# A two-layer hybrid trunk: the attention probabilities turned by VectorE instead of by TensorE, and the steps around them placed later

## The chip, the cores and the metric

The kernel runs on one core of a Trainium2 chip. The metric is the device time of one execution in microseconds (us), as the median of several. Engines are named as in the profile: PE is TensorE's matmuls, PEld its weight loads, DVE is VectorE, ACT is ScalarE, POOL is GpSimd, SP is the engine that issues the weight transfers.

## What is computed

Two layers, 256 tokens, model width 2048, everything float32. The part that matters here, per layer:

```python
h = rms_norm(x, pre_g)
proj = h @ w_in                       # 2048 x 24576: 12 mixer sections of 1536, 3 gates of 2048
o_a = dilated_mixture_attn(q_a, k_a, v_a) * silu(z_a)      # 12 heads x 128
o_c = b_c * causal_short_conv(c_c * u_c, conv_w, conv_b) * silu(z_c)
o_r = retention(q_r, k_r, v_r) * silu(z_r)                 # 12 heads x 128
merged = (sigmoid(g_a) * (o_a @ w_branch_a) + sigmoid(g_c) * (o_c @ w_branch_c)
          + sigmoid(g_r) * (o_r @ w_branch_r))
x = x + rms_norm(merged @ w_out, post_g)
```

The mixture of three dilated attentions is computed as one softmax over all keys, with the logarithm of how many of the three patterns hold a pair added to its score. For one head that is a causal 256 x 256 matrix, kept as three blocks of 128 x 128: queries 0 to 127 on keys 0 to 127, and queries 128 to 255 on both halves of the keys.

## The kernel before

**Weights.** All weights stream through SBUF once a layer, in blocks of 512 columns. A block of `w_in` is 16 tiles of 128 rows. The unit of the whole schedule is a *half*: two such tiles, 128 x 1024 numbers. Each half is split into two fp32r parts, whose sum is the float32 weight: ScalarE copies the rounded value into `w_lead` (L644), VectorE subtracts to get the rest into `w_trail` (L824). TensorE then multiplies lead by lead, lead by trail and trail by lead for both tiles of tokens (`multiply`, L585 to L587), 12 matmuls a half. There are four slots of lead and trail: the lead of half h+4 may be written when TensorE has done half h, and TensorE needs its trail when it has done half h+3.

**Order.** Each engine runs the same list of halves, and everything else is hung on it by hand: a table gives for each piece of side work the half behind which it is issued (`PE_DUE`, `ACT_DUE`, `DVE_DUE`), counted from the first half of its group. A group is four heads, and it has four blocks of B = 8 halves: for attention and retention v, q, k, z. There are three groups for a mixer and layer. ScalarE and VectorE have their tables shifted by `AHEAD` = 4: what is due at h stands there behind the split of half h+4, which is the one that can begin when TensorE has finished half h. `EVICT_DUE` says in the same way when a finished block leaves its PSUM bank; a block that ends with half h is evicted there at h, before the side work of the same half. Each engine executes strictly in this order, so a wait holds up everything behind it.

**Attention, for one group.** Queries and keys are turned (their 128 x 128 tiles transposed) by VectorE in squares of 32 x 32: 16 instructions of 32 x 256 numbers in six pieces of 3, 3, 3, 3, 2 and 2 (`TURNS`), one piece a half: q from 2B, k from 3B to 3B+5. Behind half 3B+6 TensorE multiplies the scores (L511, L512); VectorE scales them, adds the logarithms and takes the maxima (L926, L934, L936). ScalarE takes the exponentials (L694), behind the Sigmoids of the z block (L662). Behind half 4B+4 TensorE turns the probabilities with twelve transposes (L526) and ScalarE copies them to `probsT` (L701). Behind 4B+6 TensorE multiplies them with the values (L539 to L542). VectorE scales the result with the gate into `z_sb`, turns that into `qT`, and ScalarE and VectorE write lead and trail of the group's output (L715, L1014). 4B and later is the next group's first block.

**Retention** has the same steps without exponentials: rotated q and k, scores behind 3B+6 (L516, L517), masked by VectorE straight into `probsT` (L929), values behind 4B+2.

The results of the side work lie in four PSUM banks that are used in turn (`side_ready`, `drained`).

Of the kernel before, what the change touches and what calls it, by code (L numbers as in the profile page):

```python
# [14 lines left out]
P = 128  # L15
# [29 lines left out]
GATES_AT = 12 * GROUPS  # L45


STEPS = {"attention": HPB + HPB + HPB // 2,
         "conv": 0,
         "retention": HPB + HPB // 2}  # L50
X_STEPS = TILES * KT // HPB
# [98 lines left out]
def pieces(what, at):  # L150
# [1 line left out]


PE_DUE = due({
    "attention": [("scores", 3 * B + 6), ("probs", 4 * B + 4), ("values", 4 * B + 6)],
    "conv": [],
    "retention": [("scores", 3 * B + 6), ("values", 4 * B + 2)]})
ACT_DUE = due({
    "attention": [("exp", 3 * B + 7), ("probs", 4 * B + 4), ("out", 5 * B + 4)],
    "conv": [("out", 4 * B + 6)],  # L160
    "retention": [("square", 4 * B + 2), ("out", 5 * B + 2)]}, AHEAD)
DVE_DUE = due({
    "attention": pieces("q", 2 * B) + pieces("k", 3 * B) + [("scores", 3 * B + 6), ("sums", 4 * B + 3),
                 ("values", 4 * B + 6)] + pieces("z", 4 * B + 7) + [("out", 5 * B + 5)],
    "conv": pieces("prod", 2 * B) + [("conv0", 2 * B + 6), ("conv1", 2 * B + 7), ("conv2", 3 * B),
             ("gate", 4 * B)] + pieces("z", 4 * B + 1) + [("product", 4 * B + 6), ("out", 4 * B + 7)],
    "retention": pieces("q", 2 * B) + pieces("k", 3 * B) + [("scores", 3 * B + 6), ("values", 4 * B + 2),
                  ("norm", 4 * B + 3), ("gate", 4 * B + 4)] + pieces("z", 4 * B + 5) + [("out", 5 * B + 3)]}, AHEAD)

EVICT_DUE = {FIRST_HALF[n + 1] - 1 + AHEAD: n for n in range(NBLOCKS - 1)}  # L170

SQUARES_FROM = B
EVICT_DUE[SQUARES_FROM + OUT_BLOCKS + 2] = EVICT_DUE.pop(FIRST_HALF[1] - 1 + AHEAD)
# [8 lines left out]
def build(nc, x, xT, w_in, w_attention, w_conv, w_retention, w_out, post_g, params, consts, out):  # L182
# [10 lines left out]
    with ExitStack() as ctx:  # L193
# [104 lines left out]
        q_turned = sem("q_turned")  # L298
        k_turned = sem("k_turned")
        prod_turned = sem("prod_turned")  # L300
        z_turned = sem("z_turned")
        o_squared = sem("o_squared")
        o_ssq_ready = sem("o_ssq_ready")
# [61 lines left out]

        def turned(l, what, mixer, g):

            if what == "prod":
                return prod_turned, len(TURNS) * (l * GROUPS + g + 1)
            if what == "z":  # L370
                return z_turned, len(TURNS) * (l * 3 * GROUPS + group_no[mixer, g] + 1)
            i = GROUPS * (mixer == "retention") + g
            return {"q": q_turned, "k": k_turned}[what], len(TURNS) * (l * 2 * GROUPS + i + 1)
# [18 lines left out]
            return slice(h * P, (h + 1) * P)  # L392

        def out_source(mixer, t):
            return heads4(work2[:, t, :]) if mixer == "conv" else qT[:, :, tok(t)]

        def heads4(ap):
            return ap.rearrange("p (h c) -> p h c", h=HPB)
# [93 lines left out]
        def _(pe):  # L492
# [7 lines left out]
            def side_steps(l, what, mixer, g):  # L500
                m = step0(mixer, g)
                n0 = first_block(mixer, g)
                if what == "scores":
                    pe.wait_ge(*turned(l, "q", mixer, g))
                    pe.wait_ge(*turned(l, "k", mixer, g))
                    for h in range(HPB):
                        s = m + h
                        pe.wait_ge(*side_bank_free(l, s))
                        if mixer == "attention":

                            pe.matmul(side(s)[:, 0:P], qT[:, h, 0:P], kT[:, h, 0:P], start=True, stop=True)  # L511
                            pe.matmul(side(s)[:, P:3 * P], qT[:, h, P:SEQ], kT[:, h, :],  # L512
                                      start=True, stop=True).then_inc(side_ready, 1)
                        else:

                            pe.matmul(side(s)[:, 0:SEQ], kT[:, h, 0:P], qT[:, h, :], start=True, stop=True)  # L516
                            pe.matmul(side(s)[:, SEQ:3 * P], kT[:, h, P:SEQ], qT[:, h, P:SEQ],  # L517
                                      start=True, stop=True).then_inc(side_ready, 1)
                elif what == "probs":
                    pe.wait_ge(tables_in, 16)  # L520
                    for h in range(HPB):
                        s = m + HPB + h
                        pe.wait_ge(exp_ready, l * (HPB * GROUPS) + (HPB * g + h + 1))
                        pe.wait_ge(*side_bank_free(l, s))
                        for i in range(3):
                            last = pe.transpose(side(s)[:, head(i)], probs[:, h, head(i)], ident)  # L526
                        last.then_inc(side_ready, 1)
                elif what == "values":

                    pe.wait_ge(*moved_out(l, n0))  # L530
                    s0 = m + STEPS[mixer] - HPB // 2
                    for i in range(HPB):
                        pe.wait_ge(*step_drained(l, s0 - HPB + i))
                    for i in range(HPB // 2):
                        pe.wait_ge(*side_bank_free(l, s0 + i))
                        for hh in range(2):
                            h = 2 * i + hh
                            o = side(s0 + i)[:, 2 * hh * P:(2 * hh + 2) * P]
                            pe.matmul(o[:, 0:P], probsT[:, h, 0:P], v_sb[:, 0, head(h)], start=True, stop=True)  # L539
                            pe.matmul(o[:, P:2 * P], probsT[:, h, P:2 * P], v_sb[:, 0, head(h)],  # L540
                                      start=True, stop=False)
                            last = pe.matmul(o[:, P:2 * P], probsT[:, h, 2 * P:3 * P], v_sb[:, 1, head(h)],  # L542
                                             start=False, stop=True)
                        last.then_inc(side_ready, 1)
# [54 lines left out]
            for l in range(DEPTH):  # L599
                for h in range(HALVES - EARLY):  # L600
                    if l > 0 and h < EARLY:
                        continue
                    multiply(l, h)
                    for what, mixer, g in PE_DUE.get(h, []):
                        side_steps(l, what, mixer, g)
                    if h in MERGE_DUE:
                        j = MERGE_DUE[h]
                        pe.wait_ge(*merged_tiles(l, TILES * (OUT_BLOCKS + j + 1)))
                        for t in range(TILES):
                            transposes(l, MERGE_STEP0 + TILES * j + t,  # L610
                                       [merged[:, t, head(HPB * j + i)] for i in range(HPB)])
# [25 lines left out]
        def _(act):  # L637
# [9 lines left out]
            def evict(l, n):  # L647
# [3 lines left out]
                if kind == "mix":  # L651
                    copy_to = {("attention", "v"): v_sb, ("attention", "q"): q_sb, ("attention", "k"): k_sb,
                               ("conv", "u"): v_sb, ("conv", "b"): k_sb}.get((mixer, role))
                    if copy_to is not None:
                        act.wait_ge(*done_block(l, n))
                        for t in range(TILES):
                            act.activation(copy_to[:, t, :], bank(n, t)[:, :], ACT.Copy,
                                           scale=x_rstd[:, t:t + 1]).then_inc(evicted[n % 2], 1)
# [28 lines left out]
            def side_work(l, what, mixer, g):  # L687
                m = step0(mixer, g)
                if what == "exp":
                    act.wait_ge(neg_max_ready, l * GROUPS + (g + 1))  # L690
                    for h in range(HPB):
# [2 lines left out]
                            last = act.activation(probs[:, h, cols], probs[:, h, cols], ACT.Exp,  # L694
                                                  bias=neg_max[:, c:c + 1], accum_out=row_sum[:, c:c + 1])
                        last.then_inc(exp_ready, 1)
                elif what == "probs":
                    for h in range(HPB):
                        s = m + HPB + h
                        act.wait_ge(*step_ready(l, s))  # L700
                        act.activation(probsT[:, h, :], side(s)[:, 0:3 * P], ACT.Copy).then_inc(drained[s % SIDE_BANKS], 1)  # L701
                elif what == "square":
                    s0 = m + STEPS[mixer] - HPB // 2
                    for i in range(HPB // 2):
# [113 lines left out]
        def _(dve):  # L818
# [97 lines left out]
            def side_work(l, what, mixer, g):  # L916
                m = step0(mixer, g)
                n0 = first_block(mixer, g)
                if what[:-1] in ("q", "k", "prod", "z"):
                    turn(l, what[:-1], mixer, g, int(what[-1]))  # L920
                elif what == "scores":
                    for h in range(HPB):
# [94 lines left out]
            def turn(l, what, mixer, g, piece):  # L1017

                n0 = first_block(mixer, g)
                src = {"q": q_sb, "k": k_sb, "prod": q_sb, "z": z_sb}[what]  # L1020
                if what == "prod":
                    dst, done = prodT[:, :, 2:], prod_turned
                else:
                    dst, done = {"q": (qT, q_turned), "k": (kT, k_turned), "z": (qT, z_turned)}[what]
                if piece == 0:
                    before = l * 3 * GROUPS + group_no[mixer, g]
                    if before > 0:
                        dve.wait_ge(out_trail, TILES * before)
                    if what == "z" and mixer == "attention":
                        for i in range(HPB // 2):  # L1030
                            dve.wait_ge(*step_drained(l, step0(mixer, g) + STEPS[mixer] - HPB // 2 + i))
                    elif what == "z" and mixer == "conv":
# [7 lines left out]
                a, b = TURNS[piece]  # L1040
                for n in range(a, b):
                    i, j = n // QUADS, n % QUADS
                    rows = src[SQ * i:SQ * (i + 1), :, :].rearrange("p t (h x) -> p t h x", h=HPB)
                    turned_to = dst[SQ * j:SQ * (j + 1), :, :].rearrange("p h (t x) -> p t h x", t=TILES)
                    last = dve.transpose(turned_to[:, :, :, SQ * i:SQ * (i + 1)], rows[:, :, :, SQ * j:SQ * (j + 1)])  # L1045
                last.then_inc(done, 1)

# [156 lines left out]
```

## Time and profile before

| | |
|---|---|
| median of three runs | 2788.71 us (2786.34 to 2789.78) |
| profiled execution, its own time | 2791.59 us |
| its span, first to last instruction | 2789.7 us |
| TensorE busy | 2753.0 us, 99% |
| VectorE busy | 1845.4 us, 66% |
| ScalarE busy | 1229.3 us, 44% |
| mean granted TensorE clock | 0.997 |
| weight splits on VectorE (L824) | 975 of 1225 ns |
| moved over DMA | 529.11 MB, 190 GB/s |

Busy is the time in which an engine had at least one instruction in work; matmuls overlap each other, so one lasts longer (390 ns) than the distance to the next. "Idle before" in a group or timeline row is how long the engine had nothing to do ahead of it, and behind the arrow stands what the profile takes for the end of it; "issue" means that it sees no releaser. The granted clock is TensorE's, as a share of full speed (2.4 GHz).

### The profile page before, as it was taken

Reading aid. Unit: us, or ns where it says so; the run is one execution under the profiler, and the core shown is the slowest. Engines: PE = TensorE matmul, PEld = TensorE weight load, DVE = VectorE, ACT = ScalarE, POOL = GpSimd, SP = SyncE. Lnnn points to the kernel's source line nnn. Section 1 sums busy time; section 2 is a strip of 40 time slices with the busy share of each in tenths; the row PEclk is TensorE's granted clock in tenths of the full one; section 3 lists DMA queues with packets and bytes.
Section 4 is the critical chain, followed back from the end, with each engine's and each line's share of the span. In section 5 each row is a group of like instructions: output and inputs, shape, how many; then the busy total and the mean of one; then the engine's idle time right before and its main releaser. Section 6 shows DMA issues by size and latency. Waiting matters only on the chain.

```text
span 2789.7 us, 30530 instructions
## 1 busy us (share of the span) xinstructions
PE 2753.0 (99%) x12360; PEld 2282.8 (82%) x12360; DVE 1845.4 (66%) x2431; ACT 1229.3 (44%) x1426; POOL 28.2 (1%) x35
## 2 busy tenths in 40 slices
PE   8999999999999999999999999999999999999998
PEld 7888888888888878888878888888888888788887
DVE  5677644767655797746567776447776557877464
ACT  5454544444443333344454545444444433343443
POOL 0000000000000000000000000000000000000000
PEclk9999999999999999999999999999999999999999
DMA  8555556555555555556565555565655564555663
GB/s 312 174 173 195 167 196 196 190 191 194 196 196 193 167 184 170 171 200 213 181 227 178 178 187 167 195 196 182 202 192 194 196 196 156 192 169 171 204 211 136
DMA packets 264108, 529.11 MB, mean 190 GB/s; under 512 B 8352, under 2 KB 8480, under 8 KB 263712
## 3 DMA queue, kind: packets, MB, share of 16 engines
q1 hardware_dynamic: 260208, 517.24, 56.4%
q10 hardware_dynamic: 2752, 5.05, 0.5%
q0 software_dynamic: 1008, 4.87, 0.5%
q8 instruction: 97, 1.59, 0.2%
q14 instruction: 43, 0.35, 0.0%
HBM read 522.94 MB, written 4.19 MB: 189 GB/s over the span
## 4 chain that ended last, share of the span: by engine, by line
PE 98%; issue 1%; DVE 0%; DMA 0%; ACT 0%; DVEq 0%; POOL 0%; ACTq 0%; POOLq 0%
PE ps L585 32%; PE ps L587 32%; PE ps L586 32%; PE ps L516 1%; PE ps L539 0%; PE ps L542 0%; PE ps L540 0%; PE ps L512 0%; PE ps L497 0%; PE ps L526 0%; PE ps L517 0%; PE ps L511 0%; DMA merged<-xT 0%; DVE gates L1082 0%; DVE hT_trail L1054 0%
## 5 line engine op out<-in xcount | busy, mean ns | idle before, releaser
L824 DVE TENSOR_TENSOR w_trail<-raw,w_lead 128x1024 fp32r<-128x1024 f32 x975 | 1191.6, 1225 | 885.1 <-ACT w_lead L644 877.8
L644 ACT ACTIVATE w_lead<-raw 128x1024 fp32r<-128x1024 f32 x975 | 1029.9, 1060 | 1455.7 <-PE ps L587 1445.9
L585 PE MATMUL ps<-w_lead,hT_lead 128*128 128x512 f32 x3328 | 1301.3, 391 | 10.2 <-DVE w_trail L1091 8.7
L587 PE MATMUL ps<-w_lead,hT_trail 128*128 128x512 f32 x3328 | 1296.1, 389 | 0.0
L586 PE MATMUL ps<-w_trail,hT_lead 128*128 128x512 f32 x3328 | 1295.8, 389 | 0.0
L585 PEld LDWEIGHTS ps<-w_lead,hT_lead 128*128 128x128 f32 x3328 | 625.7, 188 | 141.6 <-DVE hT_trail L1073 8.6
L587 PEld LDWEIGHTS ps<-w_lead,hT_trail 128*128 128x128 f32 x3328 | 625.4, 188 | 130.3
L586 PEld LDWEIGHTS ps<-w_trail,hT_lead 128*128 128x128 f32 x3328 | 625.8, 188 | 128.5
L585 PE MATMUL ps<-w_lead,oT_lead 128*128 128x512 f32 x576 | 224.6, 390 | 0.0
L587 PE MATMUL ps<-w_lead,oT_trail 128*128 128x512 f32 x576 | 224.2, 389 | 0.0
L586 PE MATMUL ps<-w_trail,oT_lead 128*128 128x512 f32 x576 | 224.1, 389 | 0.0
L1045 DVE STREAM_TRANSPOSE qT<-z_sb 32x256 f32<-32x256 f32 x288 | 125.5, 436 | 5.3
L587 PEld LDWEIGHTS ps<-w_lead,oT_trail 128*128 128x128 f32 x576 | 108.1, 188 | 22.6
L585 PEld LDWEIGHTS ps<-w_lead,oT_lead 128*128 128x128 f32 x576 | 108.2, 188 | 22.2
L586 PEld LDWEIGHTS ps<-w_trail,oT_lead 128*128 128x128 f32 x576 | 108.2, 188 | 22.2
L1045 DVE STREAM_TRANSPOSE kT<-k_sb 32x256 f32<-32x256 f32 x192 | 83.6, 436 | 3.5
L1045 DVE STREAM_TRANSPOSE qT<-q_sb 32x256 f32<-32x256 f32 x192 | 83.6, 436 | 3.5
L1045 DVE STREAM_TRANSPOSE prodT<-q_sb 32x256 f32<-32x256 f32 x96 | 41.8, 436 | 1.8
L516 PE MATMUL ps<-qT,kT 128*128 128x256 f32 x48 | 19.6, 501 | 14.9 <-issue 14.9
L715 ACT ACTIVATE oT_lead<-qT 128x512 fp32r<-128x512 f32 x24 | 13.8, 624 | 38.5 <-DVE qT L1045 38.5
L670 ACT ACTIVATE gates<-ps,stat 128x512 f32<-128x512 f32 x48 | 30.0, 674 | 0.0
L859 DVE SCALAR_TENSOR_TENSOR z_sb<-ps,stat,z_sb 128x512 f32<-128x512 f32 x36 | 25.3, 745 | 3.9 <-ACT z_sb L662 3.9
(92 smaller groups left out, 751.9 us busy)
## 6 DMA issues: line engine op xcount, KB each, us to landing
raw<-w_in SPq DMA_DIRECT2D x383, 1024.0 KB, 5.1
raw<-w_out SPq DMA_DIRECT2D x32, 1024.0 KB, 5.1
raw<-w_branch_a SPq DMA_DIRECT2D x24, 1024.0 KB, 5.1
raw<-w_branch_c SPq DMA_DIRECT2D x24, 1024.0 KB, 5.0
raw<-w_branch_r SPq DMA_DIRECT2D x24, 1024.0 KB, 5.0
gates<-x SPq DMA_DIRECT2D x4, 512.0 KB, 14.0
post_gain<-post_norm_g POOLq DMA_DIRECT2D x2, 1024.0 KB, 6.3
gates<-x ACTq DMA_DIRECT2D x4, 512.0 KB, 5.7
```

What stands on the lines that cost most here:

```text
L516: pe.matmul(side(s)[:, 0:SEQ], kT[:, h, 0:P], qT[:, h, :], start=True, stop=True)
L585: pe.matmul(acc, lead[:, k, tok(t)], wl, start=(k == 0), stop=False)
L586: pe.matmul(acc, lead[:, k, tok(t)], wt, start=False, stop=False)
L587: last = pe.matmul(acc, trail[:, k, tok(t)], wl, start=False, stop=(k == BLOCKS[n][2] - 1))
L644: act.activation(w_lead[:, h % SPLIT_SLOTS, :], raw[:, i % RAW_SLOTS, part:part + HALF * COLS], ACT.Copy).then_inc(lead_ready, 1)
L670: act.activation(gates[:, t, COLS * j:COLS * (j + 1)], bank(n, t)[:, :], ACT.Sigmoid, scale=x_rstd[:, t:t + 1]).then_inc(evicted[n % 2], 1)
L715: act.activation(dst, out_source(mixer, t), ACT.Copy).then_inc(out_lead, 1)
L824: dve.tensor_tensor(w_trail[:, s, :], raw[:, i % RAW_SLOTS, part:part + HALF * COLS], w_lead[:, s, :].bitcast(F32), ALU.subtract).then_inc ...
L859: dve.scalar_tensor_tensor(z_sb[:, t, :], bank(n, t)[:, :], x_rstd[:, t:t + 1], z_sb[:, t, :], ALU.mult, ALU.mult).then_inc(evicted[n % 2], 1)
L1045: last = dve.transpose(turned_to[:, :, :, SQ * i:SQ * (i + 1)], rows[:, :, :, SQ * j:SQ * (j + 1)])
```

## The change

The probabilities are turned by VectorE, straight from `probs` into `probsT`: 16 instructions of 32 x 384 numbers a group, in the same six pieces, from 4B+4 to 4B+9. TensorE's transposes, ScalarE's copies and their four PSUM steps a group go away. What follows is placed later:

| | before | after |
|---|---|---|
| attention: scores | 3B+6 | 4B |
| attention: exponentials | 3B+7 | 4B+1 |
| attention: probabilities | 4B+4 | 4B+4 to 4B+9 |
| attention: values | 4B+6 | 5B+2 |
| attention: z turned | 4B+7 on | 5B+3 on |
| attention: output, ScalarE and VectorE | 5B+4, 5B+5 | 6B, 6B+1 |
| retention: scores and all behind them | 3B+6 on | each one half later |

Since the values are used later, the next group's v block (and the conv's first u block) is evicted three halves later and behind a wait for the value matmuls. z of attention and retention is turned into `kT` instead of `qT`; with that the query squares of a later group of the same mixer don't wait for the output of the one before.

```diff
-STEPS = {"attention": HPB + HPB + HPB // 2,
+STEPS = {"attention": HPB + HPB // 2,
...
 PE_DUE = due({
-    "attention": [("scores", 3 * B + 6), ("probs", 4 * B + 4), ("values", 4 * B + 6)],
+    "attention": [("scores", 4 * B), ("values", 5 * B + 2)],
     "conv": [],
-    "retention": [("scores", 3 * B + 6), ("values", 4 * B + 2)]})
+    "retention": [("scores", 3 * B + 7), ("values", 4 * B + 3)]})
 ACT_DUE = due({
-    "attention": [("exp", 3 * B + 7), ("probs", 4 * B + 4), ("out", 5 * B + 4)],
+    "attention": [("exp", 4 * B + 1), ("out", 6 * B)],
...
 DVE_DUE = due({
-    "attention": pieces("q", 2 * B) + pieces("k", 3 * B) + [("scores", 3 * B + 6), ("sums", 4 * B + 3),
-                 ("values", 4 * B + 6)] + pieces("z", 4 * B + 7) + [("out", 5 * B + 5)],
+    "attention": pieces("q", 2 * B) + pieces("k", 3 * B) + [("scores", 4 * B), ("sums", 4 * B + 3)]
+                 + pieces("probs", 4 * B + 4) + [("values", 5 * B + 2)] + pieces("z", 5 * B + 3) + [("out", 6 * B + 1)],
...
+VALUES_LATE = 3
+for _n in [first_block("attention", g) for g in range(1, GROUPS)] + [first_block("conv", 0)]:
+    EVICT_DUE[FIRST_HALF[_n + 1] - 1 + AHEAD + VALUES_LATE] = EVICT_DUE.pop(FIRST_HALF[_n + 1] - 1 + AHEAD)
...
         def out_source(mixer, t):
-            return heads4(work2[:, t, :]) if mixer == "conv" else qT[:, :, tok(t)]
+            return heads4(work2[:, t, :]) if mixer == "conv" else zT(mixer)[:, :, tok(t)]
+
+        def zT(mixer):
+            return qT if mixer == "conv" else kT
...
-                elif what == "probs":
-                    pe.wait_ge(tables_in, 16)
-                    for h in range(HPB):
-                        s = m + HPB + h
-                        pe.wait_ge(exp_ready, l * (HPB * GROUPS) + (HPB * g + h + 1))
-                        pe.wait_ge(*side_bank_free(l, s))
-                        for i in range(3):
-                            last = pe.transpose(side(s)[:, head(i)], probs[:, h, head(i)], ident)
-                        last.then_inc(side_ready, 1)
...
-                    for i in range(HPB):
-                        pe.wait_ge(*step_drained(l, s0 - HPB + i))
+                    if mixer == "attention":
+                        pe.wait_ge(*turned(l, "probs", mixer, g))
+                    else:
+                        for i in range(HPB):
+                            pe.wait_ge(*step_drained(l, s0 - HPB + i))
...
+                        before = {("attention", "v"): j - 1, ("conv", "u"): GROUPS - 1 if j == 0 else -1}.get((mixer, role), -1)
+                        if before >= 0:
+                            act.wait_ge(*step_ready(l, step0("attention", before + 1) - 1))
...
-                elif what == "probs":
-                    for h in range(HPB):
-                        s = m + HPB + h
-                        act.wait_ge(*step_ready(l, s))
-                        act.activation(probsT[:, h, :], side(s)[:, 0:3 * P], ACT.Copy).then_inc(drained[s % SIDE_BANKS], 1)
...
                 if piece == 0:
-                    before = l * 3 * GROUPS + group_no[mixer, g]
+                    before = l * 3 * GROUPS + group_no[mixer, 0 if what == "q" else g]
                     if before > 0:
                         dve.wait_ge(out_trail, TILES * before)
-                    if what == "z" and mixer == "attention":
+                    if what == "probs":
+                        dve.wait_ge(exp_ready, l * (HPB * GROUPS) + HPB * (g + 1))
...
+                    if what == "probs":
+                        rows = src[SQ * i:SQ * (i + 1), :, :].rearrange("p h (c x) -> p h c x", c=3)
+                        turned_to = dst[SQ * j:SQ * (j + 1), :, :].rearrange("p h (c x) -> p h c x", c=3)
```

## Rows read from the trace of the kernel before

**Rows 1.** The page's chain that ended last, share of the span by engine
```profile
PE 98%; issue 1%; DVE 0%; DMA 0%; ACT 0%; DVEq 0%; POOL 0%; ACTq 0%; POOLq 0%
```

**Rows 2.** Timeline of TensorE, an attention group: start us, us, instruction
```profile
190.58 0.39 PE L587 MATMUL ps<-w_lead,hT_trail 128*128 128x512 f32 x1
191.63 0.46 PE L511 MATMUL ps<-kT,qT 128*128 128x128 f32 x2 [0.66 <-issue]
...
194.14 0.58 PE L585 MATMUL ps<-w_lead,hT_lead 128*128 128x512 f32 x1
194.56 0.39 PE L586 MATMUL ps<-w_trail,hT_lead 128*128 128x512 f32 x1
...
207.72 0.39 PE L587 MATMUL ps<-w_lead,hT_trail 128*128 128x512 f32 x1
208.11 0.50 PE L585 MATMUL ps<-w_lead,hT_lead 128*128 128x512 f32 x1
...
210.99 1.47 PE L526 MATMUL ps<-cst,probs 128*128 128x128 f32 x12
212.22 0.48 PE L585 MATMUL ps<-w_lead,hT_lead 128*128 128x512 f32 x1
212.53 0.39 PE L586 MATMUL ps<-w_trail,hT_lead 128*128 128x512 f32 x1
```

**Rows 3.** Timeline of the same group, ScalarE and then VectorE
```profile
191.06 1.06 ACT L644 ACTIVATE w_lead<-raw 128x1024 fp32r<-128x1024 f32 x1 [1.72 <-PE ps L587]
...
198.35 1.28 ACT L662 ACT_TABLE_LOAD   x1
...
200.93 1.28 ACT L694 ACT_TABLE_LOAD   x1
...
205.75 3.89 ACT L644 ACTIVATE w_lead<-raw 128x1024 fp32r<-128x1024 f32 x4
...
193.29 1.94 DVE L926 SCALAR_TENSOR_TENSOR probs<-ps,cst 128x384 f32<-128x384 f32 x4
...
196.91 0.41 DVE L936 TENSOR_REDUCE stat<-probs 128x1 f32<-128x256 f32 x1
...
206.83 4.63 DVE L824 TENSOR_TENSOR w_trail<-raw,w_lead 128x1024 fp32r<-128x1024 f32 x4 [5.05 <-ACT w_lead L644]
```

**Rows 4.** Timeline of TensorE and VectorE, the first retention group
```profile
946.22 0.39 PE L587 MATMUL ps<-w_lead,hT_trail 128*128 128x512 f32 x1
...
946.85 1.23 DVE L824 TENSOR_TENSOR w_trail<-raw,w_lead 128x1024 fp32r<-128x1024 f32 x1
948.10 0.89 DVE L1045 STREAM_TRANSPOSE kT<-k_sb 32x256 f32<-32x256 f32 x2
...
949.10 0.67 PE L516 MATMUL ps<-qT,kT 128*128 128x256 f32 x2 [2.48 <-issue]
...
953.38 0.48 PE L585 MATMUL ps<-w_lead,hT_lead 128*128 128x512 f32 x1
```

**Rows 5.** TensorE's waits: waited for, us in total, times, longest
```profile
PE ps L516 <- issue: 14.9, 6, 2.5
```

**Rows 6.** Windows, two groups: length, five engines' busy us, granted clock, DMA
```profile
949.10:953.10 4.00, 4.00 (x14) 3.50 (x15) 2.55 (x4) 0.00 (x0) 0.00 (x0) 0.58 0.83 262
...
1045.90:1048.40 2.50, 2.50 (x15) 2.29 (x16) 2.40 (x4) 0.00 (x0) 0.00 (x0) 1.00 0.90 274
```

**Rows 7.** Timeline of TensorE, the second retention group
```profile
1045.90 0.67 PE L516 MATMUL ps<-qT,kT 128*128 128x256 f32 x2 [2.48 <-issue]
...
1048.51 0.47 PE L585 MATMUL ps<-w_lead,hT_lead 128*128 128x512 f32 x1
```

**Rows 8.** Groups by form: count, busy us, mean ns of one, idle before
```profile
L1045 DVE STREAM_TRANSPOSE kT<-k_sb 32x256 f32<-32x256 f32 x192 | 83.6, 436 | 3.5
...
L849 DVE TENSOR_TENSOR q_sb<-probs 128x512 f32<-128x512 f32 x12 | 8.3, 692 | 0.4
...
L662 ACT ACT_TABLE_LOAD x5 | 6.4, 1283 | 0.1
```

More of the change, by code:

```diff
@@ L154 @@
 PE_DUE = due({
-    "attention": [("scores", 3 * B + 6), ("probs", 4 * B + 4), ("values", 4 * B + 6)],
+    "attention": [("scores", 4 * B), ("values", 5 * B + 2)],
     "conv": [],
-    "retention": [("scores", 3 * B + 6), ("values", 4 * B + 2)]})
+    "retention": [("scores", 3 * B + 7), ("values", 4 * B + 3)]})
 ACT_DUE = due({
-    "attention": [("exp", 3 * B + 7), ("probs", 4 * B + 4), ("out", 5 * B + 4)],
+    "attention": [("exp", 4 * B + 1), ("out", 6 * B)],
     "conv": [("out", 4 * B + 6)],
-    "retention": [("square", 4 * B + 2), ("out", 5 * B + 2)]}, AHEAD)
+    "retention": [("square", 4 * B + 3), ("out", 5 * B + 3)]}, AHEAD)
 DVE_DUE = due({
-    "attention": pieces("q", 2 * B) + pieces("k", 3 * B) + [("scores", 3 * B + 6), ("sums", 4 * B + 3),
-                 ("values", 4 * B + 6)] + pieces("z", 4 * B + 7) + [("out", 5 * B + 5)],
+    "attention": pieces("q", 2 * B) + pieces("k", 3 * B) + [("scores", 4 * B), ("sums", 4 * B + 3)]
+                 + pieces("probs", 4 * B + 4) + [("values", 5 * B + 2)] + pieces("z", 5 * B + 3) + [("out", 6 * B + 1)],
     "conv": pieces("prod", 2 * B) + [("conv0", 2 * B + 6), ("conv1", 2 * B + 7), ("conv2", 3 * B),
              ("gate", 4 * B)] + pieces("z", 4 * B + 1) + [("product", 4 * B + 6), ("out", 4 * B + 7)],
-    "retention": pieces("q", 2 * B) + pieces("k", 3 * B) + [("scores", 3 * B + 6), ("values", 4 * B + 2),
-                  ("norm", 4 * B + 3), ("gate", 4 * B + 4)] + pieces("z", 4 * B + 5) + [("out", 5 * B + 3)]}, AHEAD)
+    "retention": pieces("q", 2 * B) + pieces("k", 3 * B) + [("scores", 3 * B + 7), ("values", 4 * B + 3),
+                  ("norm", 4 * B + 4), ("gate", 4 * B + 5)] + pieces("z", 4 * B + 6) + [("out", 5 * B + 4)]}, AHEAD)
 EVICT_DUE = {FIRST_HALF[n + 1] - 1 + AHEAD: n for n in range(NBLOCKS - 1)}
+VALUES_LATE = 3
+for _n in [first_block("attention", g) for g in range(1, GROUPS)] + [first_block("conv", 0)]:
+    EVICT_DUE[FIRST_HALF[_n + 1] - 1 + AHEAD + VALUES_LATE] = EVICT_DUE.pop(FIRST_HALF[_n + 1] - 1 + AHEAD)
 SQUARES_FROM = B
@@ L300, in build @@
         prod_turned = sem("prod_turned")
+        probs_turned = sem("probs_turned")
         z_turned = sem("z_turned")
@@ L366, in turned @@
         def turned(l, what, mixer, g):
+            if what == "probs":
+                return probs_turned, len(TURNS) * (l * GROUPS + g + 1)
             if what == "prod":
@@ L608, in _ @@
                         pe.wait_ge(*merged_tiles(l, TILES * (OUT_BLOCKS + j + 1)))
+                        pe.wait_ge(tables_in, 16)
                         for t in range(TILES):
@@ L918, in side_work @@
                 n0 = first_block(mixer, g)
-                if what[:-1] in ("q", "k", "prod", "z"):
+                if what[:-1] in ("q", "k", "prod", "probs", "z"):
                     turn(l, what[:-1], mixer, g, int(what[-1]))
@@ L1019, in turn @@
                 n0 = first_block(mixer, g)
-                src = {"q": q_sb, "k": k_sb, "prod": q_sb, "z": z_sb}[what]
-                if what == "prod":
+                src = {"q": q_sb, "k": k_sb, "prod": q_sb, "z": z_sb, "probs": probs}[what]
+                if what == "probs":
+                    dst, done = probsT, probs_turned
+                elif what == "prod":
                     dst, done = prodT[:, :, 2:], prod_turned
                 else:
-                    dst, done = {"q": (qT, q_turned), "k": (kT, k_turned), "z": (qT, z_turned)}[what]
+                    dst, done = {"q": (qT, q_turned), "k": (kT, k_turned), "z": (zT(mixer), z_turned)}[what]
                 if piece == 0:
-                    before = l * 3 * GROUPS + group_no[mixer, g]
+                    before = l * 3 * GROUPS + group_no[mixer, 0 if what == "q" else g]
                     if before > 0:
                         dve.wait_ge(out_trail, TILES * before)
-                    if what == "z" and mixer == "attention":
+                    if what == "probs":
+                        dve.wait_ge(exp_ready, l * (HPB * GROUPS) + HPB * (g + 1))
+                    elif what == "z" and mixer == "attention":
                         for i in range(HPB // 2):
@@ L1042, in turn @@
                     i, j = n // QUADS, n % QUADS
-                    rows = src[SQ * i:SQ * (i + 1), :, :].rearrange("p t (h x) -> p t h x", h=HPB)
-                    turned_to = dst[SQ * j:SQ * (j + 1), :, :].rearrange("p h (t x) -> p t h x", t=TILES)
+                    if what == "probs":
+                        rows = src[SQ * i:SQ * (i + 1), :, :].rearrange("p h (c x) -> p h c x", c=3)
+                        turned_to = dst[SQ * j:SQ * (j + 1), :, :].rearrange("p h (c x) -> p h c x", c=3)
+                    else:
+                        rows = src[SQ * i:SQ * (i + 1), :, :].rearrange("p t (h x) -> p t h x", h=HPB)
+                        turned_to = dst[SQ * j:SQ * (j + 1), :, :].rearrange("p h (t x) -> p t h x", t=TILES)
                     last = dve.transpose(turned_to[:, :, :, SQ * i:SQ * (i + 1)], rows[:, :, :, SQ * j:SQ * (j + 1)])
```

## The prediction

> **What bounds the kernel now.** I read the page first, for the chain that ended last. It is TensorE nearly from end to end [rows 1], so neither VectorE's load nor ScalarE's counts by itself: the time is the number of TensorE's instructions times their pitch, plus each hole in its queue. Next I read TensorE's instructions in order of time and looked for every place where two neighbouring weight matmuls start further apart than their pitch. From 194.14 to 207.72 there are 59 steps in 13.58 us; without the slow restart of 0.19 that is 0.227 us each, so a half of 12 matmuls takes 2.72 us [rows 2]. The places with more are few, and the change touches most of them:
> - Attention scores: the next matmul was due at 190.81 and the scores began at 191.63, a wait of 0.83 us. The whole step costs 3.33 us over the pitch and 0.19 in the restart [rows 2]. Without the wait that is 2.69.
> - Attention probabilities: the twelve transposes cost 1.23 us from start to start, and 0.08 in the restart behind them [rows 2]: 1.31.
> - A stumble at 208.11: 0.16 us late, and I add a restart of 0.08 [rows 2]. This is a weight half whose trail VectorE had ready only then, behind ScalarE's exponentials [rows 3].
> - Retention scores: due at 946.45, begun at 949.10: 2.65 us lost [rows 4]. What ended it was the last two key squares, which VectorE began at 948.10 and ended at 948.99; the trace calls it "issue" because it names no releaser. All six groups lose the same (14.9 us of idle time in six waits, [rows 5]; the pipeline's drain comes on top).
> - After that hole the granted clock was 0.58 in one group and 1.00 in the next [rows 6]. At full speed the score matmuls took 2.61 us, from 1045.90 to 1048.51 [rows 7]; at the lower level (1.2 GHz for most of the stretch, against 2.4) 4.28 us, from 949.10 to 953.38 [rows 4]. Four of the six groups are of the slow kind. With their restarts they cost 1.62 us more on average.
>
> **What goes away.** Transposes 6 x 1.31 = 7.9 us. The wait before attention scores, 6 x 0.83 = 5.0: the scores come two halves later and the key squares don't. The stumble, 5 x 0.24 = 1.2 (one group, layer two's first, has no table load before its Sigmoid, [rows 8] has five for six groups, and doesn't stumble). The wait before retention scores, 6 x 2.65 = 15.9: one half later TensorE is due at 946.45 + 2.72 = 949.17, and the squares end at 948.99. That leaves under 0.1 us for the semaphore; I charge 0.5 for six. The slow clock behind it, 4 x 1.62 = 6.5. Together 36.5 us. ScalarE's 24 copies and the drained banks go too, hidden behind TensorE before and after.
>
> **What comes in: 96 VectorE transposes of 32x384.** The trace has only 32x256, 436 ns [rows 8]. Lower bound: the same 436. Upper bound: in proportion, 654. Between them: a subtraction of 1024 columns takes 1225 ns [rows 3, 4] and an addition of 512 takes 692 [rows 8], 1.04 ns for a column and about 0.16 us for the instruction. The short transpose fits that (0.16 + 0.27 = 0.43), so 128 more columns give 436 + 133 = 0.57 us. I take 0.57.
>
> The skill speaks for more speed: the Trainium skill, "VectorE: DVE Perf Modes", section "The three transpose paths", gives 311 ns for a whole 128x128 in bf16 on VectorE. By it a group's twelve squares of 128 would take 3.7 us, VectorE would never be late, and the sum would be 2752 us. The trace has eight such tiles in f32 in 16 x 0.436 = 7.0 us [rows 8], so I don't use it.
>
> These transposes are 55 us in all. VectorE has room for that on average; the question is the six stretches where they must be done before TensorE's value matmuls. I lay out one, with 0 at the end of half 4B, where scores are now issued (B is 8 halves).
> - TensorE: scores, then halves. Half 4B+n ends at 2.69 + 2.72n. The value matmuls come behind half 4B+10, due at 2.69 + 27.2 - 0.16 (a matmul's drain, 0.39 against the pitch) = 29.7.
> - ScalarE: half 4B-1 ended at -2.72, its lead copy runs to -1.6, then table load and two Sigmoids take 2.58 (198.35 to 200.93, [rows 3]) to 1.0. Only then comes the lead of 4B+4, to 2.05.
> - VectorE: trail of 4B+4 to 3.3; score scaling and maxima 4.03 us (193.29 to 196.91 + 0.41, [rows 3]) to 7.3.
> - ScalarE: exponentials with their table load, 4.82 us (200.93 to 205.75, [rows 3]), 7.35 to 12.2. Behind them three lead copies are queued: 13.25, 14.2, 15.15 (0.97 each, [rows 3]).
> - VectorE: trails of 4B+6 and 4B+7 to 15.6 (1.16 each, [rows 3]), reciprocal to 15.75, trail of 4B+8 to 17.0. TensorE needs 4B+6 at 16.15 and has it at 14.5: no stumble. The probabilities begin at 17.0, where an unburdened VectorE would begin at 16.0.
> - From there it is never idle: 16 transposes at 0.57, five trails at 1.25 between them (946.85 to 948.10, [rows 4]), 0.04 for each of six pieces: 9.12 + 6.25 + 0.24 = 15.6, done at 32.6.
>
> A piece of three with its trail takes 3.0 us where TensorE uses a half in 2.72. So TensorE starts values at 32.7 where 29.7 was due: **a new wait of 3.0 us**. Layer two's first group lacks the Sigmoid's table load; the same steps start the squares at 16.1 and give 2.1. Together 5 x 3.0 + 2.1 = 17.1 us. The wait is as long as the one that retention loses, so I carry over what followed that one: slow clock in four groups, 4 x 1.62 = 6.5 (bounds 0 and six, 9.7).
>
> The other moves cost nothing. The first two groups' next value block is evicted three halves later; ScalarE waits there for the value matmuls (to about 35.4 in the count above) and is done at 36.8, before half 4B+11 ends at 38. That block's bank is wanted again only five halves after that. If values came 2 us later still, the eviction would touch the next lead copy, which has four halves in hand. The gate transposes now fill kT instead of qT, so the next group's query squares wait for no output; at 6B VectorE has both (3.5 us in a half) and at 6B+1 the outputs, about 2 us behind, against 5 to 6 us before a trail would be late. Retention's scores now meet the z eviction in VectorE's order: both are done 6.1 us after half 4B-1, and the next lead copy is ready at 6.5.
>
> **Sum.** -36.5 + 17.1 + 6.5 + 0.5 = -12.4 us. The profiled execution's span is 2789.7 and its own time 2791.6, 2.9 above the median of the three runs, 0.1%; I take the sum off the median: 2788.7 - 12.4 = 2776.3.
>
> **The rivals.**
> - *The new wait is nearly hidden.* With 436 ns a transpose the squares end 2.1 us earlier: wait 0.8, none in layer two's first group, and no slow clock, since the 0.83 us hole of today has none behind it. -36.5 + 4.2 + 0.5 = -31.8: 2757. For it: most of an instruction could be start-up. Against it: the slope above.
> - *Gain and loss cancel.* With 654 ns they end 1.3 us later: wait 4.3 (3.4 in the one group), 24.9 in all, slow clock in all six, 9.7. -36.5 + 24.9 + 9.7 + 0.5 = -1.4: 2787. For it: the pieces already overrun the half, so every nanosecond counts 16 times.
> - *Slower.* The same wait, if a transpose of three blocks a head costs more than its share. The sum turns positive when the wait passes 4.55 us, from 0.67 us a transpose. At 0.75 it is 5.9 (5.0): 34.5 + 9.7 + 0.5 - 36.5 = +8: 2797. For it: no three-block transpose is in the trace. Against it: no VectorE row costs more than its share.
>
> **How the numbers follow.** Chances: my forecast 0.62, nearly hidden 0.18, cancel 0.12, slower 0.08. Within the forecast the clock moves the time from 2770 (never slow) to 2779 (always), and 0.03 us on the transpose moves it by 3 either way: its own range is 2766 to 2783. The range for all is 2757 to 2787; it leaves out half of the nearly hidden case below, and the slower one and a little above. 0.2% is 5.6 us, about what a measurement of this kernel can tell from no change, so faster means under 2783.1: forecast and hidden, 0.80; the cancelling case is "same", 0.12; slower 0.08.
>
> **What the next profile would show.** No transposes of probs on TensorE. Retention scores with no idle time before them and granted clock 1.00: right if the key squares were the releaser, and if 2.5 us still stand there, that step is wrong. TensorE idle some 2.8 us before the value matmuls of attention in five groups, less in the sixth; transposes into probsT near 570 ns. No late trail at 4B+6. The prediction falls if the transposes' duration is off (16 times that a group), or if the slow clock follows more or fewer of the waits.

## The result and the profile after

| | before | after |
|---|---|---|
| median of four runs | 2787.83 us (2786.34 to 2789.78) | 2766.72 us (2766.23 to 2767.30) |
| span of the profiled execution | 2789.7 us | 2764.7 us |
| VectorE busy | 1845.4 us | 1899.0 us |
| ScalarE busy | 1229.3 us | 1221.4 us |

The ratio is 0.9924, with a 95% interval of 0.9907 to 0.9941: faster by 21 us in the medians and by 25 us between the two profiled executions. The forecast was 12.4 us less, 2776.3, with a range from 2757 to 2787. The direction and the range held; the gain is 1.7 times the forecast. Among the runs below, one of e2's eleven (3797 us) and one of e4's five (3898 us) are slow ones, with a mean granted clock of 0.68 and 0.67, and the ratios leave them out.

The page of the changed kernel: TensorE's busy time, the chain that ended last by engine, and the new group of transposes.

```profile
PE 2735.2 (99%) x12288; PEld 2269.5 (82%) x12288; DVE 1899.0 (69%) x2527; ACT 1221.4 (44%) x1402; POOL 27.5 (1%) x35
...
PE 98%; SPq 1%; issue 1%; DMA 1%; DVE 0%; ACT 0%; DVEq 0%; POOL 0%; POOLq 0%
...
L1056 DVE STREAM_TRANSPOSE probsT<-probs 32x384 f32<-32x384 f32 x96 | 54.7, 569 | 1.7
```

TensorE is the chain, as in [rows 1]. The transposes into `probsT` take 569 ns, where the prediction had 570. VectorE is busy for 54 us more in all, and that alone costs nothing; what costs is where the work stands, as the next rows show.

TensorE's waits (waited for; us in total, times, longest):

```profile
PE ps L543 <- issue: 10.8, 6, 1.8
...
PE ps L589 <- DVE w_trail L827: 1.2, 2, 0.7
```

The wait of [rows 5] is gone and another stands in its place: six times 1.8 us before L543, the first value matmul. The second row is a late trail, in two places in this execution (33.1 and 1385.4 us; before it was one place, 0.5 us); neither is at the exponentials, where the stumble is gone.

TensorE in the first retention group, to be read against [rows 4]:

```profile
947.30 0.39 PE L591 MATMUL ps<-w_lead,hT_trail 128*128 128x512 f32 x1
947.53 0.59 PE L526 MATMUL ps<-qT,kT 128*128 128x256 f32 x2
...
950.07 0.47 PE L589 MATMUL ps<-w_lead,hT_lead 128*128 128x512 f32 x1
```

The scores follow the last weight matmul by 0.23 us, the pitch. From 947.30 to 950.07 the step costs 2.54 us over the pitch, where before it was 6.93. In four of the six groups TensorE still waits for 0.1 us there, 0.4 us in all, where 0.5 was charged. And TensorE around an attention group's value matmuls:

```profile
225.23 0.39 PE L591 MATMUL ps<-w_lead,hT_trail 128*128 128x512 f32 x1
227.42 0.46 PE L543 MATMUL ps<-v_sb,probsT 128*128 128x128 f32 x2 [1.80 <-issue]
...
230.09 0.47 PE L589 MATMUL ps<-w_lead,hT_lead 128*128 128x512 f32 x1
```

They were due at 225.46 (225.23 and the pitch) and began at 227.42: 1.96 us lost. This difference between due and begun is called a hole from here on; it is 0.16 us longer than the idle time in the row. Both kinds of step in windows (length, busy us of PE, PEld, DVE, ACT and POOL with counts, granted clock, DMA share, GB/s):

```profile
227.40:230.00 2.60, 2.58 (x23) 2.60 (x24) 2.03 (x5) 0.00 (x0) 0.00 (x0) 1.00 0.93 310
947.50:950.00 2.50, 2.50 (x16) 2.29 (x16) 2.29 (x3) 2.21 (x3) 0.00 (x0) 1.00 0.93 283
```

Granted clock 1.00 behind the new hole as well; in the other five groups too the value matmuls took the 2.67 us of full speed.

### The profile page after: what moved, and what is told of

Same layout as the page of the kernel before. It is cut to its first block, busy times and chain, and to the rows that moved or that the text cites. A ratio compares the mean times of both kernels' runs of the same rounds, so it can differ in the third digit from the quotient of the medians.

```text
span 2764.7 us, 30431 instructions
## 1 busy us (share of the span) xinstructions
PE 2735.2 (99%) x12288; PEld 2269.5 (82%) x12288; DVE 1899.0 (69%) x2527; ACT 1221.4 (44%) x1402; POOL 27.5 (1%) x35
## 4 chain that ended last, share of the span: by engine, by line
PE 98%; SPq 1%; issue 1%; DMA 1%; DVE 0%; ACT 0%; DVEq 0%; POOL 0%; POOLq 0%
PE ps L589 32%; PE ps L591 32%; PE ps L590 32%; DMA raw<-w_in 1%; PE ps L543 0%; PE ps L526 0%; PE ps L544 0%; PE ps L546 0%; PE ps L522 0%; PE ps L507 0%; SPq L445 0%; PE ps L527 0%; PE ps L521 0%; DVE w_trail L827 0%; SPq L417 0%
## 5 line engine op out<-in xcount | busy, mean ns | idle before, releaser
L1056 DVE STREAM_TRANSPOSE kT<-z_sb 32x256 f32<-32x256 f32 x192 | 83.7, 436 | 3.5
L1056 DVE STREAM_TRANSPOSE probsT<-probs 32x384 f32<-32x384 f32 x96 | 54.7, 569 | 1.7
L1056 DVE STREAM_TRANSPOSE qT<-z_sb 32x256 f32<-32x256 f32 x96 | 41.8, 436 | 1.8
L718 ACT ACTIVATE oT_lead<-kT 128x512 fp32r<-128x512 f32 x24 | 13.8, 625 | 38.5 <-DVE kT L1056 38.5
```

The source lines that it names most:

```text
L718: act.activation(dst, out_source(mixer, t), ACT.Copy).then_inc(out_lead, 1)
```

## The experiments

Due times are again halves from a group's start, B = 8. All medians below have their interval against the kernel before, run beside them. The changed kernel was not run again beside them: differences to it are taken to its 2766.72 us, and the spans of the profiled executions bear them out (e1 is 3.1 us longer, e3 12.2 and e4 4.0 us shorter). "Slow clock" is a granted clock of 0.50, 1.2 GHz; a value between 0.50 and 1.00 in a window is a mean of both levels.

### e1: retention's half alone

```diff
 # PE, on the kernel before
-    "retention": [("scores", 3 * B + 6), ("values", 4 * B + 2)]})
+    "retention": [("scores", 3 * B + 7), ("values", 4 * B + 3)]})
 # and one later for all of retention behind it, on ScalarE and VectorE
```

> The kernel before, with only retention's scores and all behind them one half later. Theory K (the wait for the key squares and the slow clock behind it are most of the gain): the six holes of 2.5 us go, granted clock 1.00 in the score matmuls, 22 us less than before, about 2766. Rival A (most of the gain is attention's: transposes off TensorE): at most 10 us less than before, 2778 or more. Rival M (the wait isn't for the key squares and moves along): no change, 2788.

Measured: 2769.57 us, ratio 0.9928 (0.9915 to 0.9940), 20.6 us less than the before beside it (2790.20). Moving retention's scores by one half, with TensorE's transposes in place, gives most of the change's gain: between the profiled executions 21.9 us of 25.0 (spans 2789.7 and 2767.8). Theory K holds; A and M are out. In TensorE's waits the retention line is gone and the one before attention's scores is left:

```profile
PE ps L511 <- issue: 4.0, 6, 0.7
```

### e2: all but retention's half

```diff
 # PE, on the changed kernel
-    "retention": [("scores", 3 * B + 7), ("values", 4 * B + 3)]})
+    "retention": [("scores", 3 * B + 6), ("values", 4 * B + 2)]})
```

> The changed kernel with retention's due times as they were before. Theory K: the holes before retention's scores are back, 22 us more than the changed kernel, 2789, within 3 us of the kernel before, since in attention 14.5 us saved (transposes 7.9, wait before scores 5.4, late trail 1.2) stand against a new wait of 2.0 us in six groups, 12. Rival A: 2770 to 2778, clearly faster than before.

Measured: 2785.86 us, ratio 0.9986 (0.9977 to 0.9995), 4.3 us less than before. The expectation was 2789 and at most 3 us less than before. One slow group fewer in its trace, 1.6 us, is part of that. So the part for which the change is named, with its own moves, is worth about 3 us: 2.7 us are left here without that group, and the spans of e1 and of the changed kernel, neither with a slow group, differ by 3.1. Both holes are in this trace, retention's old one and the new one:

```profile
PE ps L526 <- issue: 14.9, 6, 2.5
PE ps L543 <- issue: 10.8, 6, 1.8
```

Of the six retention holes three were followed by the slow clock here, against four in the trace of the kernel before, with the same 2.5 us of idle time.

### e3: the values one half later

```diff
 # on the changed kernel
-    "attention": [("scores", 4 * B), ("values", 5 * B + 2)],
+    "attention": [("scores", 4 * B), ("values", 5 * B + 3)],
 # z squares, outputs and v eviction behind them one half later too
-VALUES_LATE = 3
+VALUES_LATE = 4
```

> The changed kernel with attention's values, and z squares, output and v eviction behind them, one half later (5B+3). Theory W (the wait before the values is the probability squares' lateness, 2.0 us, less than a half of 2.72): the six waits go and nothing takes their place, 12 us less than the changed kernel, 2755. Rival V (VectorE is the bound of this stretch, so the wait comes back elsewhere: late trails, or the z squares and outputs that now meet the next group's query squares): less than 4 us gained, 2763 or more, with holes before the weight matmuls around 6B.

Measured: 2754.35 us, ratio 0.9874 (0.9860 to 0.9887): 12.4 us less than the changed kernel, as Theory W had it; Rival V is out. This is the fastest kernel of the study. TensorE at the first value matmul, with no wait:

```profile
226.00 0.40 PE L591 MATMUL ps<-w_lead,hT_trail 128*128 128x512 f32 x1
226.23 0.39 PE L543 MATMUL ps<-v_sb,probsT 128*128 128x128 f32 x2
```

VectorE in the same stretch and on to the next group's query squares:

```profile
224.20 1.16 DVE L1056 STREAM_TRANSPOSE probsT<-probs 32x384 f32<-32x384 f32 x2
...
245.13 0.89 DVE L1056 STREAM_TRANSPOSE kT<-z_sb 32x256 f32<-32x256 f32 x2
246.05 1.33 DVE L1056 STREAM_TRANSPOSE qT<-q_sb 32x256 f32<-32x256 f32 x3
...
252.88 1.29 DVE L1017 TENSOR_TENSOR oT_trail<-kT,oT_lead 128x512 fp32r<-128x512 f32 x2
```

The last probability squares end at 225.36, 0.9 us ahead of 226.23. At 245.13 and 246.05 z squares and query squares now share halves. VectorE has no idle time from there until 250.9, and TensorE doesn't notice: it waits for no trail there.

### e4: the moves without the transposes

```diff
 # e1 with, on PE and ScalarE (VectorE's "scores" move to 3 * B + 7 likewise)
-    "attention": [("scores", 3 * B + 6), ("probs", 4 * B + 4), ("values", 4 * B + 6)],
+    "attention": [("scores", 3 * B + 7), ("probs", 4 * B + 4), ("values", 4 * B + 6)],
...
-    "attention": [("exp", 3 * B + 7), ("probs", 4 * B + 4), ("out", 5 * B + 4)],
+    "attention": [("exp", 4 * B), ("probs", 4 * B + 4), ("out", 5 * B + 4)],
```

> The kernel before with TensorE still turning the probabilities; only retention one half later and attention's scores and exponentials one half later (3B+7, 4B). Theory K: 22 us from retention and 6 x 0.9 = 5.4 us from attention's scores, and the late trail of 1.2 us grows or stays: 2760 to 2762, faster than the changed kernel by 5 us, so that turning on VectorE, with its new wait, brought less than the plain moves. Rival A: without taking the transposes off TensorE no gain beyond the changed kernel's: 2770 or more. Rival X: the exponentials, later against the trails, make TensorE wait for more than 1 us a group: 2766 or more.

Measured: 2762.59 us, ratio 0.9902 (0.9887 to 0.9918), just above the 2760 to 2762 of Theory K; A and X are out. That is 4 us faster than the changed kernel, with TensorE turning the probabilities as before. TensorE at the second group's scores and at the transposes behind the exponentials, with no wait at either:

```profile
192.21 0.39 PE L587 MATMUL ps<-w_lead,hT_trail 128*128 128x512 f32 x1
192.44 0.38 PE L511 MATMUL ps<-kT,qT 128*128 128x128 f32 x2
...
208.44 0.39 PE L587 MATMUL ps<-w_lead,hT_trail 128*128 128x512 f32 x1
208.67 1.47 PE L526 MATMUL ps<-cst,probs 128*128 128x128 f32 x12
```

Against e1 it is 7.0 us less, where 5.4 from the scores and 1.2 from the stumble at the exponentials were to be had; in its trace both are gone. e3 is e4 with the probabilities turned by VectorE and no hole before the values, 8.2 us less: the price of the transposes on TensorE, forecast at 7.9.

### e5 and e6: more squares in the last piece

```diff
 # on the changed kernel; EXTRA = 2 in e5, 4 in e6
+                    for m in range(EXTRA if what == "probs" and n == 15 else 0):
+                        spare_to = spare[SQ * m:SQ * (m + 1), :, :].rearrange("p h (c x) -> p h c x", c=3)
+                        last = dve.transpose(spare_to, rows[:, :, :, SQ * j:SQ * (j + 1)])
```

> The changed kernel with two more transposes of 32x384 a group in the last piece, into a buffer that nobody reads: 1.14 us more VectorE work before the values, the only thing changed. The wait grows from 2.0 to 3.1 us a group, so this is the hole that the prediction had forecast for the changed kernel. Theory W (the wait is VectorE's lateness one for one) without the slow clock: 6 x 1.14 = 6.8 us more, 2773.5. With the slow clock in four groups as the prediction had it: 13 us more, 2780. Rival V (slack hides it): no change, 2767.

Measured: 2776.22 us, ratio 0.9964 (0.9952 to 0.9976), single runs from 2774.39 to 2784.15. The profiled execution is the longest of them (span 2782.3). TensorE around the first group's values (the added lines shift the line numbers by two):

```profile
131.09 0.39 PE L593 MATMUL ps<-w_lead,hT_trail 128*128 128x512 f32 x1
134.44 0.77 PE L545 MATMUL ps<-v_sb,probsT 128*128 128x128 f32 x2 [2.96 <-issue]
...
139.56 0.77 PE L591 MATMUL ps<-w_lead,hT_lead 128*128 128x512 f32 x1
```

The hole is 3.12 us (134.44 less the due 131.32), 1.16 more than in the changed kernel for 1.14 us of VectorE work: one for one. The value matmuls took 5.12 us there, not 2.67. The six groups' windows, columns as above:

```profile
134.40:139.50 5.10, 5.05 (x24) 5.09 (x25) 2.33 (x5) 0.00 (x0) 0.00 (x0) 0.50 0.39 148
232.90:237.10 4.20, 4.13 (x23) 4.16 (x24) 2.31 (x5) 0.00 (x0) 0.00 (x0) 0.61 0.49 181
330.10:332.70 2.60, 2.60 (x23) 2.60 (x24) 2.03 (x5) 0.00 (x0) 0.00 (x0) 1.00 0.72 274
1518.80:1523.10 4.30, 4.29 (x24) 4.30 (x25) 2.30 (x5) 0.00 (x0) 0.00 (x0) 0.60 0.45 170
1616.00:1621.10 5.10, 5.08 (x24) 5.10 (x25) 2.31 (x5) 0.00 (x0) 0.00 (x0) 0.50 0.38 144
1714.40:1718.60 4.20, 4.17 (x25) 4.20 (x25) 2.31 (x5) 0.00 (x0) 0.00 (x0) 0.62 0.46 173
```

Holes of the same length, and the granted clock behind them is at 0.50 in two groups, near 0.6 in three and at 1.00 in one. The shortest run is 7.7 us above the changed kernel, nearly what the holes alone cost (6.8 to 7.0); the profiled one is 17.6 above.

> The same with four more transposes: hole 4.3 us a group. One for one and full clock: 13.7 us more, 2780.5. If a hole of this length always brings the slow clock, 1.62 us a group more: 2790. If the slow clock costs nothing here (128-column matmuls paced by something else): 2780.5 with a granted clock near 0.5 in the value matmuls.

Measured: 2792.56 us, ratio 1.0018 (1.0008 to 1.0028): slower than the kernel before. The holes are 4.29 us, again one for one:

```profile
PE ps L545 <- issue: 24.8, 6, 4.1
```

In all six groups the value matmuls ran slow, 1.5 to 2.5 us more each. Against the changed kernel the longer holes cost 14.0 us (6 x 2.33) and the clock 13.2, read from the six steps; the medians differ by 25.8.

### e7: the values one half early

```diff
 # on the changed kernel, PE only
-    "attention": [("scores", 4 * B), ("values", 5 * B + 2)],
+    "attention": [("scores", 4 * B), ("values", 5 * B + 1)],
```

> The changed kernel with only TensorE's value matmuls one half earlier (5B+1), all of VectorE's and ScalarE's order as it is. The squares are ready at the same point of VectorE's queue, so the hole grows by a half, 2.0 + 2.72 = 4.7 us: 16 us more, 2783, and with the slow clock in all six groups 2793. Rival: VectorE runs ahead in step with the earlier issue, and the hole is the same: 2767.

Measured: 2792.64 us, ratio 1.0019 (1.0009 to 1.0028), against the 2793 expected with six slow groups; the rival, a hole that stays the same, is out. The hole is 4.68 us in the trace, forecast at 4.7, and all six are followed by the slow clock (1.7 us each in five, 2.1 in one):

```profile
PE ps L543 <- issue: 27.1, 6, 4.5
```

With e3 that makes a series: values one half early, as placed, one half late give holes of 4.7, 2.0 and 0 us, at the same readiness of the squares.

## Why the prediction was right in direction and short in size

| term, us | forecast | by the trace after |
|---|---|---|
| TensorE's transposes | -7.9 | -7.9 |
| wait before attention scores, 6 | -5.0 | -5.4 |
| late trail at the exponentials | -1.2 | -1.2 |
| retention scores: wait, clock, remainder | -21.9 | -22.1 |
| new wait before the values, 6 | +17.1 | +12.1 |
| slow clock behind it | +6.5 | 0 |
| sum | -12.4 | -24.5 |

The right column is each step's excess over the pitch, read in the trace after and set against the same step before. The two spans differ by 25.0.

**Right.** That TensorE's queue is the time, so that only holes and removed instructions count; that retention's wait was for the key squares (in all six groups of before TensorE starts 0.1 us after the last of them ends) and vanishes with one half (e1 alone shows it, and e2 by its return); the price of the new transposes, 569 ns, taken from the slope of other VectorE instructions and not in proportion (654); the price of TensorE's transposes (e3 against e4); that a new wait stands before the values, and that it is paid in full (e5, e6, e7). The rule set aside in the prediction (the Trainium skill, "VectorE: DVE Perf Modes", "The three transpose paths", 311 ns for a 128x128 in bf16, in blocks of 32x32) would have left no wait: here twelve f32 tiles took 16 x 0.569 = 9.1 us, 0.76 us a tile, and the wait is there.

**The step that failed: "The probabilities begin at 17.0".** In the count of the prediction, with 0 at the end of half 4B (195.79 in this trace), they began at 15.84. ScalarE in the first stretch of that group:

```profile
196.63 1.06 ACT L649 ACTIVATE w_lead<-raw 128x1024 fp32r<-128x1024 f32 x1
201.18 1.06 ACT L649 ACTIVATE w_lead<-raw 128x1024 fp32r<-128x1024 f32 x1 [3.49 <-PE ps L591]
202.25 1.28 ACT L702 ACT_TABLE_LOAD   x1
203.55 0.40 ACT L702 ACTIVATE probs<-probs,stat 128x128 f32<-128x128 f32 x1
...
207.08 1.99 ACT L649 ACTIVATE w_lead<-raw 128x1024 fp32r<-128x1024 f32 x2
209.39 1.06 ACT L649 ACTIVATE w_lead<-raw 128x1024 fp32r<-128x1024 f32 x1 [0.33 <-PE ps L591]
```

and VectorE:

```profile
202.47 0.41 DVE L939 TENSOR_REDUCE stat<-probs 128x1 f32<-128x256 f32 x1
...
208.15 2.36 DVE L827 TENSOR_TENSOR w_trail<-raw,w_lead 128x1024 fp32r<-128x1024 f32 x2 [4.14 <-ACT w_lead L649]
...
210.54 1.17 DVE L827 TENSOR_TENSOR w_trail<-raw,w_lead 128x1024 fp32r<-128x1024 f32 x1
211.63 1.72 DVE L1056 STREAM_TRANSPOSE probsT<-probs 32x384 f32<-32x384 f32 x3
213.39 1.23 DVE L827 TENSOR_TENSOR w_trail<-raw,w_lead 128x1024 fp32r<-128x1024 f32 x1
...
226.16 1.16 DVE L1056 STREAM_TRANSPOSE probsT<-probs 32x384 f32<-32x384 f32 x2
```

The prediction let ScalarE load its table behind the wait for the maxima. The maxima end at 202.88, but the load had begun at 202.25 and ran beside them: the exponentials start at 203.55, as soon as the load is over. With VectorE's maxima done 0.2 us sooner than counted, ScalarE is free at 207.08, which is 11.3 and not 12.2. That removes the backlog: the third lead copy at 209.39 stands behind an idle time of 0.33, so it waits for TensorE and no longer for ScalarE's queue, and VectorE starts the squares where an unburdened one would. From there the count held: 15.6 us forecast, 15.7 measured (211.63 to 227.32). The wait is 1.96 us, and the same in all six groups. The 2.1 us forecast for layer two's first group is nearly what all six got, because nothing but the half's end set the start. In every one of the six groups the load begins 6.5 us into the count, straight behind a lead copy (201.18 to 202.24 above), with or without the Sigmoid's load earlier on.

**The slow clock was a term of the sum that was mis-sized, 6.5 for 0.** It was carried over from a hole of 2.65 us to one of 3.0. The real hole is 2.0, and behind it the clock stayed at 1.00 in all six groups of the trace. What the forecast hole would have cost, e5 shows: with 3.1 us in six groups its median is 2776.22, against 2776.3 forecast, with five slow groups in the profiled execution and, to judge by their times, fewer in most runs. That the two agree to 0.1 us is chance: of the 9.5 us that separate e5 from the changed kernel the holes are 6.8 to 7.0, which leaves under 3 for the clock where the forecast had 6.5.

**Spans and medians.** The profiled execution of before had four slow groups, and it is one of its longer ones. Fifteen runs of before beside e1 to e4 lie between 2785.3 and 2792.0, with a mean granted clock of 0.999 in the shortest and 0.997 in the longest. The changed kernel's four lie within 1.1 us, and e3's four, with no hole over 0.2 us before side work, within 0.3. Part of what the change removes is thus a cost that only some executions pay; that would explain why 25 us between two traces are 21 in the medians. That the spread of before is due to the clock behind its six holes is inferred from this and from e2's three slow groups; single runs have no trace to show it.

## What to carry to other kernels

Where one engine's queue is the whole time, list every place where two of its instructions stand further apart than the pitch, and price a change by that list; a wait of under one unit of the schedule is worth one move of the step behind it. Here two such moves brought some 28 us without the change of engine (e4), and the change of engine brought its 8 us only when its own wait was moved away too (e3). Work on an engine with room costs nothing on average and everything at its deadline: 1 us more in front of a deadline that is already missed is 1 us in the end, for each group.

## What the runs showed of the hardware

- A table load on ScalarE began before the wait of the activation behind it was over: at 202.25, with the maxima done at 202.88. In five of the six groups 0.63 us of its 1.28 ran beside the maxima; in layer two's first group the maxima had ended 0.12 us before the load began, and nothing was hidden.
- TensorE's clock behind an idle time: at 1.8 us before the values it was never slow (12 of 12 groups of the changed kernel and e2 at full speed); at 2.48 us before retention's scores it was slow in 4 of 6 groups, and in e2 in 3 of 6; before the values again, at 3.0 us (e5) in 5 of 6, at 4.1 us (e6) and 4.5 us (e7) in all. One slow step cost 1.5 to 2.5 us more than its 2.6.
- The clock can also fall when the idle time is already over: in the first retention group of before it was 1.00 from 949.10 to 949.70, while the scores ran, and 0.50 from 949.72 to 953.10; in the first group of e5 it was 0.50 already from 133.80, ahead of the values at 134.44. The Trainium skill, "TensorE: Matmul & The Clock Gate", Part 1, says that the gate watches on a rhythm of its own, which doesn't start with the kernel. e5's trace fits that, with equal holes and unequal clocks behind them; no run here isolates it.
- A VectorE transpose of 32 partitions takes 436 ns for 256 columns and 569 for 384: 1.04 ns for a column and 0.17 us for the instruction.
